# The last two multiplications on the keys and rates of an RWKV-7 scan, on GpSimd instead of VectorE

## The chip, the cores and the metric

One core of a Trainium2 chip runs the whole program. The metric is the device time of one execution in microseconds. TensorE (PE) runs the matrix products, VectorE (DVE), ScalarE (ACT) and GpSimd (POOL) the rest, and each engine works through its own instructions in order. SyncE (SP) issues most transfers. Engines wait for each other by semaphores.

## The reference

The program is one step of a two-layer model for 128 context tokens and 512 latent tokens of width 1024. Layer 0 mixes by HGRN2 and RG-LRU, layer 1 by RWKV-7; a mixture of experts ends each layer. The change is in RWKV-7's recurrence, which runs forwards and backwards in time:

```
w  = exp(-exp(-0.5) * sigmoid(w_in));  a = sigmoid(a_in)
kd = k * (1 + (a - 1) * k_a)
step:  sa = S @ (-kk_t)
       S  = S * w_t + sa (kk_t * a_t)^T + v_t kd_t^T
       o_t = S @ r_t
```

## The kernel before, in words

The recurrence is computed in chunks of 128 tokens: 5 chunks (128 context, 4 x 128 latent) for 4 groups of 4 heads, which makes 20 scan steps, n = 0 to 19, each for both directions d = 0 and 1. A step's operands are [128 x 256] tiles in SBUF, one row for each channel of a pair of heads.

For step n the code forms the running sum of the log decays, moves it so that half of the chunk's decay lies on each side (`hb`, the step's centre), and takes exponentials of it on ACT (`E1`, `E2`, `E3`). From them come four operands: the keys `KP` = kd * `E2`, the rates `BE` = kk * a * `E2`, and the two halves of `KR`, kk * `E3` and r * `E1`. `bonus_operands` (L2059) makes kd in place of the decay sum (`KD`, L2065) and the bonus term `SQ` (L2069, twice). `decayed_operands` (L2071) then multiplies `KP` (L2076), `BE` (L2077) and the two halves of `KR` (L2079, L2080), and the last of these raises `unit_ready`.

PE uses them in `rate_products`: for each direction a PSUM tile `AR` = `BE` x `KR` (16 matmuls of 128 x 256 for the two directions, in half tiles of 64 channels), then the small tile `BN` from `SQ`. `KP` x `KR` gives `BR` a little later. DVE copies `AR` out under a mask in `rates_out` (L2111), SP writes it to DRAM and reads its 16x16 diagonal blocks back, GpSimd inverts those (L742 to L752, a chain of 32 small operations each waiting for the one before), SP stores and reloads the inverses, and PE goes from 16 to 128 in three levels (tiles `G`, `D`, L1107 waits for the first load).

The order of the work is written out by hand. In its loop, PE does for step n: `rate_products(n + 1)`, level 4 of step n, `BR`, the levels 5 and 6, then the outputs `OT`. DVE does in step n: `rates_out(n + 1)`, masks and levels of step n, between them the operands of step n + 2, at the end `bonus_operands` and `decayed_operands` of n + 2 for d = 0 and d = 1, then `outputs_taken(n)` (L2174 to L2183), and from group 1 on the normalisation of the group before (L2097 to L2103). So what DVE makes at the end of step n is what PE wants at the very start of step n + 1. PSUM is a ring of four tiles: a tile can be opened when the tile four places before it has been read out. The `AR` tile of d = 0 is four places before the second `G` tile of level 4.

Of the kernel before, what the change touches and what calls it, by code (L numbers as in the profile page):

```python
# [86 lines left out]
def scan_step(n):  # L87

    return divmod(n, NCH) if n < NGRP * NCH else None


def step_name(n):
    g, st = divmod(n, NCH)
    return f"_{g}_{st}"
# [66 lines left out]
def build(nc, A, const, outs, xspill, slots_in, slots_out):  # L161
# [3 lines left out]
    ALU = mybir.AluOpType  # L165
# [5 lines left out]
    with ctx:  # L171
# [28 lines left out]
        def vcol(name, i, n=1):  # L200
            return VT[:, VB[name] + i:VB[name] + i + n]
# [12 lines left out]
        def small(n):  # L214
# [36 lines left out]
            "lru_rows", "lru_sent", "f_log", "b_ready", "head_diff", "head_exp", "head_ready",  # L251
            "lvl_diff", "lvl_exp", "lvl_q", "lvl_k", "st_in", "s_final", "s_final_sent", "on_root", "o_a_ready",
            "chosen", "routed", "zero_ready", "zero_filled", "slots_filled", "over_done", "x_parked", "x_back", "xi_ready", "lora_in", "rw_st_in", "rw_clear", "scr_clear", "tri_in", "tri_out",
            "kk_sq", "gates_exp", "kk_norm", "decay_sum", "decay_exp", "unit_ready", "kb_t", "fin_out",
            "rhs_out", "r0_ready", "n_out", "gates_clamped", "gates_done", "ctx_state", "ctx_state_sent", "scan_done", "gn_centred", "gn_sq", "gn_var", "gn_root",
            "z_ready", "silu_out", "acc_ready", "y_sent")}
        pool_chain = sem("pool_chain")
# [156 lines left out]
        R1 = Rf.rearrange("p (k t) -> p k t", k=KT)  # L414
# [16 lines left out]
        STR = []  # L431
# [11 lines left out]
        for d in range(2):  # L443
            z = {}
# [25 lines left out]
        def square(a):  # L470
            return a.rearrange("p (i k) -> p i k", k=TB)

        def turned(a):
            return a.rearrange("p (i k) -> p k i", k=TB)
# [171 lines left out]
        def _(pool):  # L646
# [85 lines left out]
            def link(ins):  # L732
                n_chain[0] += 1
                ins.then_inc(pool_chain, 1)
                pool.wait_ge(pool_chain, n_chain[0])

            for n in range(NGRP * NCH):
                pool.wait_ge(S["tri_in"], 32 * (n + 1))
                if n:
                    for d in range(2):  # L740
                        pool.wait_ge(tri_stored[d], 32 * n)
                link(nc.gpsimd.tensor_copy(square(triL[0:NB_T]), turned(triX[0:NB_T])))  # L742
                link(nc.gpsimd.tensor_scalar(triR, triL, -1.0, None, ALU.mult))
                link(nc.gpsimd.memset(triR[:, 0::TB + 1], 1.0))
                r3, l3 = square(triR), square(triL)
                for k in range(1, TB - 1):
                    m = TB - 1 - k
                    prod = triX[:, 0:m * k].rearrange("p (i c) -> p i c", c=k)
                    link(nc.gpsimd.tensor_tensor(prod, l3[:, k + 1:, k:k + 1].broadcast_to([2 * NB_T, m, k]),
                                                 r3[:, k:k + 1, 0:k].broadcast_to([2 * NB_T, m, k]), ALU.mult))  # L750
                    link(nc.gpsimd.tensor_tensor(r3[:, k + 1:, 0:k], r3[:, k + 1:, 0:k], prod, ALU.subtract))
                nc.gpsimd.tensor_copy(square(triRT), turned(triR)).then_inc(S["tri_out"], 1)  # L752
            moe(1)


        @block.tensor
        def _(pe):
            nxt = [0]

            def open_tile(n):  # L760
                assert n == nxt[0], (n, nxt[0])
                nxt[0] += 1
                if n >= RING_P:
                    pe.wait_ge(psum_free[n % RING_P], n // RING_P)
                return tile(n)
# [173 lines left out]
            for i in range(3):  # L939
                ins = nc.tensor.transpose(ps[:, i * P:(i + 1) * P], vrow[:, i * P:(i + 1) * P], ident)  # L940
            done(ins)
            pe.wait_ge(S["x_in"], 32)
            for k in range(KT):
                ps = open_tile(T["xT"] + k)
                for c in range(NCH):
                    ins = nc.tensor.transpose(ps[:, c * P:(c + 1) * P], xtok[:, c, k * P:(k + 1) * P], ident)
# [14 lines left out]
            for u in range(8):  # L961
                c, d = u // 2, u % 2
# [120 lines left out]
            def rate_products(n):  # L1083
                for d in range(2):
                    z = STR[d]
                    pe.wait_ge(S["unit_ready"], 2 * n + d + 1)
                    ps = open_tile(T["AR" + step_name(n)] + d)
                    done(head_products(ps, z["BE"][n % 2], z["KR"][n % 3]))
                ps = open_tile(T["BN" + step_name(n)])
                for d in range(2):  # L1090
                    for j in range(UC):
                        c0 = HG * d + 2 * j
                        ins = mm(ps[:, c0:c0 + 2], STR[d]["SQ"][:, j * P:(j + 1) * P], hsel)
                done(ins)
# [168 lines left out]
        def _(act):  # L1263
# [231 lines left out]
            def decay_exps(n, d):  # L1495
                z = STR[d]
                h0 = 4 * (n % 3) + 2 * d
                act.wait_ge(S["decay_sum"], 2 * n + d + 1)
                A_(em[:, h0:h0 + 2], hb[:, h0:h0 + 2], ACT.Exp, scale=-W_DECAY)
                A_(z["E1"], z["B"], ACT.Exp, scale=-W_DECAY)  # L1500
                A_(z["E2"], z["B"], ACT.Exp, scale=W_DECAY)
                A_(z["E3"], z["E3"], ACT.Exp, scale=-W_DECAY).then_inc(S["decay_exp"], 1)
# [78 lines left out]
        def _(dve):  # L1581
# [445 lines left out]
            def sum_decays(n, d):  # L2027

                z = STR[d]
                h0 = 4 * (n % 3) + 2 * d  # L2030
                dve.wait_ge(S["gates_done"], 2 * n + d + 1)
                one = half_one[:, 0:1].broadcast_to([P, P])
                for j in range(UC):
                    js = slice(j * P, (j + 1) * P) if d == 0 else slice((j + 1) * P - 1, j * P - 1 if j else None, -1)
                    ins = nc.vector.tensor_tensor_scan(z["B"][:, js], one, z["LA"][:, js], 0.0, ALU.mult, ALU.add)
                link(ins)
                e0 = P - 1 if d == 0 else 0
                link(TS(hb[:, h0:h0 + 2], z["B"][:, e0::P], 0.5, None, ALU.mult))
# [20 lines left out]
            def bonus_operands(n, d):  # L2059

                g, st = scan_step(n)
                z, ch = STR[d], chunk_of(st, d)
                ts, cg = slice(ch * P, (ch + 1) * P), slice(UC * g, UC * (g + 1))
                dve.wait_ge(S["decay_exp"], 2 * n + d + 1)
                link(TT(c3(z["KD"]), K1[:, cg, ts], c3(z["KP"][n % 2]), ALU.mult))  # L2065
                for j in range(UC):
                    ct = UC * g + j
                    js = slice(j * P, (j + 1) * P)
                    STT(z["SQ"][:, js], R1[:, ct, ts], vcol("rw_rk", ct), z["KD"][:, js], ALU.mult, ALU.mult)  # L2069

            def decayed_operands(n, d):  # L2071

                g, st = scan_step(n)
                z, ch = STR[d], chunk_of(st, d)
                ts, cg = slice(ch * P, (ch + 1) * P), slice(UC * g, UC * (g + 1))
                TT(z["KP"][n % 2], z["KD"], z["E2"], ALU.mult)  # L2076
                TT(z["BE"][n % 2], z["BE"][n % 2], z["E2"], ALU.mult)  # L2077
                kr = z["KR"][n % 3].rearrange("p (j a t) -> p j a t", j=UC, a=2)
                TT(kr[:, :, 0, :], c3(z["KK"]), c3(z["E3"]), ALU.mult)  # L2079
                TT(kr[:, :, 1, :], R1[:, cg, ts], c3(z["E1"]), ALU.mult).then_inc(S["unit_ready"], 1)  # L2080
# [251 lines left out]
```

## Time and profile before

| | us |
|---|---|
| three runs | 2650.51, 2660.67, 2659.58 |
| their median | 2659.58 |
| the profiled execution | 2647.23 |
| its span, first to last instruction | 2645.4 |
| PE busy | 2155.2 (81%) |
| DVE busy | 1062.1 (40%) |
| ACT busy | 684.7 (26%) |
| GpSimd busy | 351.2 (13%) |
| mean granted TensorE clock | 0.896 of full speed |

The scan takes some 750 us of the span, from 1415 to about 2170 us, and there a step takes about 35 us. A row of a timeline is one instruction or a run of equal ones: its start, its length, the engine, the line of the code, the operation with its output and inputs, and in brackets how long the engine had been idle and what ended that. Matmuls show the line of the helper that issues them, L776. PEclk is the TensorE clock that was granted, as a share of full speed: 1.00 is 2.4 GHz, 0.50 is 1.2 GHz.

### The profile page before, as it was taken

The numbers are of one execution on the slowest core, as the hardware profiler recorded it, in microseconds if no ns is written. First come the engines' busy times: TensorE is split into PE (matmuls) and PEld (weight loads), VectorE is DVE, ScalarE is ACT, GpSimd is POOL, SyncE is SP. The second block draws the span as 40 slices with busy tenths as digits, with TensorE's granted clock in tenths as the row PEclk, the third lists the DMA queues.
The fourth block names the chain that finished last, engine by engine and source line by source line (L and its number), as shares of the span: only waits on it lengthen the run. The fifth ranks groups of instructions, "written<-read, shape, count | busy, mean of one in ns | idle before, by whom it ended". The sixth has DMA issues, their size and how long they took to land.

```text
span 2645.4 us, 29905 instructions
## 1 busy us (share of the span) xinstructions
PE 2155.2 (81%) x11858; PEld 1601.5 (61%) x11858; DVE 1062.1 (40%) x2278; ACT 684.7 (26%) x1402; POOL 351.2 (13%) x816
## 2 busy tenths in 40 slices
PE   6999990777885997369995999999999989759964
PEld 3554560444564674135574898888888875546742
DVE  2246221666132110271003577777777753311104
ACT  1254221222130110030003244444444421301112
POOL 3000001232001000100002122233222210010001
PEclk9999995888977998679997699999999999779987
DMA  8124319333144995421101222221222231449943
GB/s 261 48 96 159 120 62 398 114 128 119 46 144 163 344 343 183 151 88 64 64 32 33 54 52 58 50 55 40 54 55 55 48 107 33 143 172 346 343 149 127
DMA packets 328505, 337.12 MB, mean 127 GB/s; under 512 B 76836, under 2 KB 296208, under 8 KB 327856
## 3 DMA queue, kind: packets, MB, share of 16 engines
q1 hardware_dynamic: 308496, 262.61, 31.8%
q0 software_dynamic: 11984, 40.63, 4.1%
q10 hardware_dynamic: 7888, 31.99, 3.0%
q8 instruction: 95, 1.56, 0.2%
q14 instruction: 42, 0.34, 0.0%
HBM read 259.67 MB, written 75.51 MB: 127 GB/s over the span
## 4 chain that ended last, share of the span: by engine, by line
PE 71%; DVE 14%; ACT 5%; DMA 3%; issue 2%; POOL 2%; ACTq 2%; SPq 1%; POOLq 0%; DVEq 0%
PE psum_ring L776 65%; PE psum_ring L1098 2%; PE psum_ring L860 1%; DMA arena<-expert_inputs 1%; ACTq L1397 1%; ACT h_normed L1292 1%; ACTq L1394 1%; DVE arena L2069 1%; PE psum_ring L1180 1%; POOL expert_inputs L697 1%; POOL arena L709 1%; DMA arena<-expert_outputs,arena 0%; PE psum_ring L932 0%; ACT arena L1307 0%; DVE h_normed L2183 0%
## 5 line engine op out<-in xcount | busy, mean ns | idle before, releaser
L776 PE MATMUL psum_ring<-arena 128*128 128x256 f32 (+5 forms) x3440 | 645.9, 359 | 57.4 <-ACT arena L1307 18.2
L776 PEld LDWEIGHTS psum_ring<-arena 128*128 128x128 f32 (+1 forms) x3440 | 490.9, 196 | 167.9 <-issue 75.5
L776 PE MATMUL psum_ring<-arena,weight_ring 128*128 128x64 f32 (+3 forms) x1792 | 367.7, 391 | 21.4 <-DVE arena L2080 15.8
L776 PEld LDWEIGHTS psum_ring<-arena,weight_ring 128*128 128x128 f32 (+1 forms) x1792 | 245.9, 204 | 132.4 <-issue 103.8
L776 PE MATMUL psum_ring<-h_normed,weight_ring 128*128 128x512 f32 (+1 forms) x768 | 211.6, 437 | 5.8 <-ACT h_normed L1292 5.8
L776 PEld LDWEIGHTS psum_ring<-h_normed,weight_ring 128*128 128x128 f32 x768 | 117.7, 192 | 98.8 <-issue 98.8
L776 PE MATMUL psum_ring<-weight_ring,small 128*2 128x256 f32 x768 | 175.8, 387 | 0.3
L860 PE MATMUL psum_ring<-consts,arena 128*128 128x128 f32 x350 | 55.2, 295 | 105.1 <-DMA arena<-expert_inputs 102.3
L776 PE MATMUL psum_ring<-x_resid,weight_ring 128*128 128x512 f32 (+1 forms) x480 | 111.8, 390 | 25.7 <-DVE x_resid L2002 25.7
L776 PEld LDWEIGHTS psum_ring<-weight_ring,small 128*2 128x2 f32 x768 | 63.8, 86 | 101.4 <-issue 9.4
L860 PEld LDWEIGHTS psum_ring<-consts,arena 128*128 128x128 f32 x350 | 46.9, 154 | 127.0 <-DMA arena<-expert_inputs 105.0
L776 PEld LDWEIGHTS psum_ring<-x_resid,weight_ring 128*128 128x128 f32 x480 | 70.9, 199 | 65.2 <-issue 65.2
L1739 DVE COPY arena<-psum_ring 128x1024 f32<-128x1024 f32 x32 | 39.2, 1224 | 163.0 <-PE psum_ring L860 162.9
L776 PE MATMUL psum_ring<-h_normed 128*128 128x128 f32 x190 | 29.5, 309 | 87.4 <-DVE h_normed L1957 67.8
L1747 DVE TENSOR_TENSOR arena<-arena,psum_ring 128x256 f32<-128x256 f32 x32 | 13.5, 421 | 205.2 <-ACT arena L1317 205.2
L1317 ACT ACTIVATE arena<-psum_ring 128x256 f32<-128x256 f32 x32 | 12.3, 383 | 297.5 <-PE psum_ring L776 297.5
L776 PE MATMUL psum_ring<-arena,x_resid 128*128 128x64 f32 (+1 forms) x624 | 86.9, 274 | 0.2 <-DVE arena L2023 0.2
L1276 ACT ACTIVATE h_normed<-x_resid 128x640 f32<-128x640 f32 x40 | 28.7, 734 | 211.1 <-DVE x_resid L1636 205.0
L776 PEld LDWEIGHTS psum_ring<-h_normed 128*128 128x128 f32 x190 | 25.7, 213 | 92.8 <-issue 92.3
L2133 DVE TENSOR_TENSOR arena<-psum_ring,consts 128x256 f32<-128x256 f32 x120 | 49.4, 422 | 78.0 <-PE psum_ring L776 77.4
L1636 DVE SCALAR_TENSOR_TENSOR x_resid<-psum_ring,modulation,x_resid 128x128 f32<-128x128 f32 x64 | 31.6, 545 | 122.1 <-PE psum_ring L776 120.6
L776 PEld LDWEIGHTS psum_ring<-arena,x_resid 128*128 128x128 f32 x624 | 80.0, 195 | 0.3 <-issue 0.3
(361 smaller groups left out, 3142.5 us busy)
## 6 DMA issues: line engine op xcount, KB each, us to landing
arena<-in_moe_w SPq DMA_DIRECT2D x105, 1024.0 KB, 10.7
weight_ring<-in_w_mod SPq DMA_DIRECT2D x48, 1024.0 KB, 5.2
arena<-expert_inputs SPq DMA_DIRECT2D x35, 512.0 KB, 7.3
expert_outputs<-arena POOLq DMA_DIRECT2D x32, 512.0 KB, 7.7
weight_ring<-in_ab_w_in SPq DMA_DIRECT2D x14, 1024.0 KB, 5.0
expert_inputs<-arena ACTq DMA_DIRECT2D x1, 12800.0 KB, 36.4
expert_outputs<-arena ACTq DMA_DIRECT2D x1, 12800.0 KB, 67.3
weight_ring<-expert_outputs SPq DMA_DIRECT2D x20, 512.0 KB, 4.6
```

Of the source, the lines that this page charges most:

```text
L697: pool.indirect_dma_start(slots_in, bass.IndirectOffsetOnAxis(ap=PI[:, j * NCH + c:j * NCH + c + 1], axis=0), HTOK[:, c, :], None).then_in ...
L709: pool.indirect_dma_start((G0, G1)[j][:, c, :], None, slots_out, bass.IndirectOffsetOnAxis(ap=PI[:, j * NCH + c:j * NCH + c + 1], axis=0)) ...
L776: return nc.tensor.matmul(out, lhsT, rhs, start=start, stop=stop)
L860: ins = nc.tensor.transpose(ps[:, k * P:(k + 1) * P], src[:, k * P:(k + 1) * P], ident)
L1098: ins = nc.tensor.transpose(ps[:, c0 + hl * P:c0 + (hl + 1) * P], src[:, hl * P:(hl + 1) * P], ident)
L1180: ins = nc.tensor.transpose(ps[:, c0:c0 + P], STR[d][key][n % 2][:, j * P:(j + 1) * P], ident)
L1276: A_(H[:, k, :], X[:, k, :], ACT.Square).then_inc(S["sq_ready"], 1)
L1292: A_(H[:, k, a:b], H[:, k, a:b], ACT.Identity, scale=coef[i][:, 2 * k + s:2 * k + s + 1], bias=MOD[:, layer, shift + k, s:s + 1]).then_inc ...
L1394: act.dma_start(dst.rearrange("(a p) d -> p a d", p=P), ZERO.unsqueeze(1).broadcast_to([P, NE + N_OVER, D])).then_inc(S["zero_filled"], 16)
L1636: ins = STT(X[:, k, a:b], ps[:, a:b], MOD[:, layer, gate + k, s:s + 1], X[:, k, a:b], ALU.mult, ALU.add)
L1739: free(nc.vector.tensor_copy(XGT[e % 2], ps), n)
L2133: free(TT(STR[d]["G"].rearrange("p (h c) -> p h c", c=HD), ps[:, 0:HG * HD].rearrange("p (h c) -> p h c", c=HD), gm, ALU.mult), tn)
```

## The change

The multiplications that make `KP` and `BE` leave DVE's `decayed_operands`. GpSimd gets a function `decayed_keys(n)` that waits for the new semaphore `bonus_out` (raised by DVE's last bonus product of step n, direction d), multiplies `KP` and `BE` by `E2`, and raises the new semaphore `decayed`. It stands once ahead of GpSimd's loop, for step 0, and then behind the inverse of step n, for step n + 1. PE waits for `decayed` beside `unit_ready` ahead of each `AR` tile. ACT and DVE wait for `decayed` of the step before where they overwrite `E2` and `KD`.

```diff
+            def decayed_keys(n):
+                if scan_step(n):
+                    for d in range(2):
+                        z = STR[d]
+                        pool.wait_ge(S["bonus_out"], 2 * n + d + 1)
+                        nc.gpsimd.tensor_tensor(z["KP"][n % 2], z["KD"], z["E2"], ALU.mult)
+                        nc.gpsimd.tensor_tensor(z["BE"][n % 2], z["BE"][n % 2], z["E2"],
+                                                ALU.mult).then_inc(S["decayed"], 1)
+            decayed_keys(0)
             for n in range(NGRP * NCH):
...
                 nc.gpsimd.tensor_copy(square(triRT), turned(triR)).then_inc(S["tri_out"], 1)
+                decayed_keys(n + 1)
...
                     pe.wait_ge(S["unit_ready"], 2 * n + d + 1)
+                    pe.wait_ge(S["decayed"], 2 * n + d + 1)
...
                 act.wait_ge(S["decay_sum"], 2 * n + d + 1)
+                if n:
+                    act.wait_ge(S["decayed"], 2 * n + d - 1)
...
                 dve.wait_ge(S["gates_done"], 2 * n + d + 1)
+                if n:
+                    dve.wait_ge(S["decayed"], 2 * n + d - 1)
...
-                    STT(z["SQ"][:, js], R1[:, ct, ts], vcol("rw_rk", ct), z["KD"][:, js], ALU.mult, ALU.mult)
+                    ins = STT(z["SQ"][:, js], R1[:, ct, ts], vcol("rw_rk", ct), z["KD"][:, js], ALU.mult, ALU.mult)
+                ins.then_inc(S["bonus_out"], 1)
...
-                TT(z["KP"][n % 2], z["KD"], z["E2"], ALU.mult)
-                TT(z["BE"][n % 2], z["BE"][n % 2], z["E2"], ALU.mult)
```

On DVE, at the end of a scan step, the operands of a later step for d = 0 and the first instruction for d = 1 stood before as follows (L2065 is `KD`, L2069 `SQ`, L2076 `KP`, L2077 `BE`, L2079 and L2080 `KR`):

```order
L2065 TENSOR_TENSOR arena<-arena,weight_ring 128x256 [waits decay_exp]
L2069 SCALAR_TENSOR_TENSOR arena<-arena,vectors 128x128 [waits dve_chain]
L2069 SCALAR_TENSOR_TENSOR arena<-arena,vectors 128x128
L2076 TENSOR_TENSOR weight_ring<-arena 128x256
L2077 TENSOR_TENSOR weight_ring<-weight_ring,arena 128x256
L2079 TENSOR_TENSOR arena<-arena 128x2x128
L2080 TENSOR_TENSOR arena<-arena 128x2x128
L2065 TENSOR_TENSOR arena<-arena,weight_ring 128x256 [waits decay_exp]
```

The same place of DVE after the change, where the lines have moved by 16 or 17 (L2082 is `KD`, L2086 `SQ`, L2095 and L2096 `KR`):

```order
L2082 TENSOR_TENSOR arena<-arena,weight_ring 128x256 [waits decay_exp]
L2086 SCALAR_TENSOR_TENSOR arena<-arena,vectors 128x128 [waits dve_chain]
L2086 SCALAR_TENSOR_TENSOR arena<-arena,vectors 128x128
L2095 TENSOR_TENSOR arena<-arena 128x2x128
L2096 TENSOR_TENSOR arena<-arena 128x2x128
L2082 TENSOR_TENSOR arena<-arena,weight_ring 128x256 [waits decay_exp]
```

Two instructions of each direction are gone from DVE's row, and the rest keeps its order.

On GpSimd, the end of the inverse of step 0 and the beginning of that of step 1 stood before as follows (L752 is the last copy of an inverse, L742 the first of the next):

```order
L751 TENSOR_TENSOR weight_ring<-weight_ring 64x14 [waits pool_chain]
L752 COPY weight_ring<-weight_ring 64x256 [waits pool_chain]
L742 COPY weight_ring<-weight_ring 32x256 [waits tri_stored1,tri_stored0,tri_in]
L743 TENSOR_SCALAR weight_ring<-weight_ring 64x256 [waits pool_chain]
L744 MEMSET weight_ring 64x16 [waits pool_chain]
```

The same place of GpSimd after the change, with L743 and L744 now the multiplications of `KP` and `BE`, for d = 0 and then d = 1:

```order
L762 TENSOR_TENSOR weight_ring<-weight_ring 64x14 [waits pool_chain]
L763 COPY weight_ring<-weight_ring 64x256 [waits pool_chain]
L743 TENSOR_TENSOR arena<-arena 128x256 [waits bonus_out]
L744 TENSOR_TENSOR arena<-arena 128x256
L743 TENSOR_TENSOR arena<-arena 128x256 [waits bonus_out]
L744 TENSOR_TENSOR arena<-arena 128x256
L753 COPY weight_ring<-weight_ring 32x256 [waits tri_stored1,tri_stored0,tri_in]
```

The four multiplications of step 1 stand between the inverse of step 0 and that of step 1.

## Rows read from the trace of the kernel before

**Rows 1.** The chain that ended last (page, part 4), by engine

```profile
PE 71%; DVE 14%; ACT 5%; DMA 3%; issue 2%; POOL 2%; ACTq 2%; SPq 1%; POOLq 0%; DVEq 0%
```

**Rows 2.** Windows (us, busy PE PEld DVE ACT POOL, PEclk, DMA share, GB/s)

```profile
1490.00:1520.00 30.00, 29.40 (x150) 27.31 (x149) 17.55 (x45) 8.31 (x23) 0.12 (x1) 0.56 0.09 20
1580.00:1610.00 30.00, 28.46 (x253) 26.84 (x252) 21.07 (x53) 15.21 (x40) 9.60 (x32) 1.00 0.23 54
```

**Rows 3.** Waits of PE, 1640 to 2140 us (us, times, longest)

```profile
PE psum_ring L776 <- DVE arena L2111: 8.7, 7, 1.7
PE psum_ring L776 <- DVE weight_ring L2111: 5.7, 6, 1.2
...
PE psum_ring L776 <- DVE arena L2080: 2.5, 3, 0.8
```

**Rows 4.** Timeline of DVE from 2109 us (start us, us, line, operation, tiles)

```profile
2109.75 0.62 DVE L2069 SCALAR_TENSOR_TENSOR arena<-arena,vectors 128x128 f32<-128x128 f32 x2
2110.29 0.42 DVE L2076 TENSOR_TENSOR arena<-arena 128x256 f32<-128x256 f32 x1
...
2111.30 0.41 DVE L2080 TENSOR_TENSOR arena<-arena 128x256 f32<-128x256 f32 x1
...
2113.61 0.42 DVE L2080 TENSOR_TENSOR arena<-arena 128x256 f32<-128x256 f32 x1
...
2117.50 1.22 DVE L2111 TENSOR_TENSOR arena<-psum_ring,consts 128x1024 f32<-128x1024 f32 x1
```

**Rows 5.** Timeline of PE in the same stretch

```profile
2113.76 2.00 PE L776 MATMUL psum_ring<-arena 64*128 64x256 f32 x16
...
2118.86 1.08 PE L776 MATMUL psum_ring<-weight_ring 128*128 128x64 f32 x8 [1.18 <-DVE arena L2111]
```

**Rows 6.** Timeline of PE at the first step of a group

```profile
1824.84 1.13 PE L776 MATMUL psum_ring<-arena 64*128 64x256 f32 x8 [0.82 <-DVE arena L2080]
...
1828.41 1.08 PE L776 MATMUL psum_ring<-weight_ring 128*128 128x64 f32 x8 [0.52 <-DVE arena L2111]
```

**Rows 7.** GpSimd's multiplications of layer 0, line 687 (ns min/median/max)

```profile
L687 POOL TENSOR_TENSOR h_normed<-h_normed,arena x19: 852/863/5882, 453.2 to 654.0; 128x320 f32<-128x320 f32 x19
```

**Rows 8.** Timeline of GpSimd and DVE in layer 0, at 452 us

```profile
451.89 0.82 DVE L1949 TENSOR_TENSOR arena<-arena 128x640 f32<-128x640 f32 x1 [53.19 <-ACT small L1412]
...
453.19 1.03 POOL L687 TENSOR_TENSOR h_normed<-h_normed,arena 128x320 f32<-128x320 f32 x1 [187.24 <-ACT h_normed L1418]
453.23 1.67 DVE L1949 TENSOR_TENSOR arena<-arena 128x640 f32<-128x640 f32 x1
...
454.18 1.58 POOL L688 TENSOR_TENSOR h_normed<-h_normed,arena 128x320 f32<-128x320 f32 x1
454.82 1.48 DVE L1950 TENSOR_TENSOR h_normed<-h_normed,arena 128x512 f32<-128x512 f32 x1
```

**Rows 9.** Timeline of the same two engines at 510 us

```profile
510.05 0.82 DVE L1949 TENSOR_TENSOR arena<-arena 128x640 f32<-128x640 f32 x1
510.15 5.88 POOL L687 TENSOR_TENSOR h_normed<-h_normed,arena 128x320 f32<-128x320 f32 x1 [26.23 <-ACT h_normed L1418]
...
514.33 0.82 DVE L1957 TENSOR_TENSOR h_normed<-h_normed,arena 128x640 f32<-128x640 f32 x1
```

**Rows 10.** Timeline at the start of the scan, several engines

```profile
1432.97 3.78 PE L776 MATMUL psum_ring<-arena,weight_ring 64*128 64x256 f32 x16 [14.20 <-DVE arena L2080]
...
1456.72 0.68 POOL L752 COPY weight_ring<-weight_ring 64x256 f32<-64x256 f32 x1
1456.86 0.83 DVE L2076 TENSOR_TENSOR arena<-arena 128x256 f32<-128x256 f32 x1
...
1456.99 3.84 PE L776 MATMUL psum_ring<-arena 64*128 64x256 f32 x16 [14.47 <-DVE arena L2080]
...
1464.00 4.03 PE L776 MATMUL psum_ring<-weight_ring 128*128 128x64 f32 x16 [1.38 <-DMA weight_ring<-expert_outputs]
```

**Rows 11.** Window of 2 us behind a wait of PE, as Rows 2

```profile
2081.00:2083.00 2.00, 2.00 (x11) 1.80 (x12) 1.45 (x5) 0.00 (x0) 0.00 (x0) 0.50 0.70 212
```

More of the change, by code:

```diff
@@ L253, in build @@
             "chosen", "routed", "zero_ready", "zero_filled", "slots_filled", "over_done", "x_parked", "x_back", "xi_ready", "lora_in", "rw_st_in", "rw_clear", "scr_clear", "tri_in", "tri_out",
-            "kk_sq", "gates_exp", "kk_norm", "decay_sum", "decay_exp", "unit_ready", "kb_t", "fin_out",
+            "kk_sq", "gates_exp", "kk_norm", "decay_sum", "decay_exp", "unit_ready", "kb_t", "fin_out", "bonus_out", "decayed",
             "rhs_out", "r0_ready", "n_out", "gates_clamped", "gates_done", "ctx_state", "ctx_state_sent", "scan_done", "gn_centred", "gn_sq", "gn_var", "gn_root",
```

## The prediction

> **What bounds the kernel now.** I read the chain of waits first. PE is 71% of it and DVE 14% [rows 1], so a microsecond of DVE counts only where PE waits for it. The windows come next: in a scan step at full clock PE is busy 28.46 of 30 us, and there are stretches at half clock where it is busy throughout [rows 2]; nothing on DVE matters in those. The list of PE's waits then shows where DVE is late at the point that the change touches: 8.7 + 5.7 = 14.4 us in 13 waits for L2111, the masked copy that frees an `AR` tile, and 2.5 us in 3 waits for L2080, the last operand [rows 3]. Over 20 steps the whole place is worth 17 us, 0.6% of the program, if the clock is left aside.
>
> The timeline of one step shows how the two hang together [rows 4, 5]. DVE makes the operands of d = 0 and d = 1 without a gap, the last ending at 2113.61 + 0.42 = 2114.03. PE begins the `AR` products at 2113.76; its 16 matmuls take 2.00 us, so those of d = 1 begin 1.00 us later, at 2114.76, and find their operands 0.73 us old. The operands are not what PE waits for. But behind them on DVE stand the outputs, the normalisation and L2111 at 2117.50, and for that one PE waits 1.18 us at 2118.86. DVE has no pause of its own choice in this stretch but one for ACT, so a microsecond more or less ahead of the outputs moves L2111 by as much. This is the form of the steps from group 1 on. At the first step of a group PE arrives sooner: it waits 0.82 us for L2080 itself and then 0.52 us for L2111 [rows 6]. In the steps of group 0 no normalisation stands in between, and neither wait is there.
>
> **What the change takes away.** Four multiplications a step leave DVE (two for each direction). Starts 2110.29 and 2111.30 are three instructions apart [rows 4], so one costs 0.335 us and four 1.34 us.
>
> **What it adds.** Four multiplications a step on GpSimd, of 128x256. The trace shows none of that size there; the nearest row is layer 0's multiplication of 128x320, 863 ns in the middle [rows 7]. By size that is 863 x 256/320 = 690 ns. The bounds of one are 0.69 us by itself and 5.88 us, the longest of that row.
>
> Where these stand is the question, since GpSimd works while DVE makes the other operands. Layer 0 shows the two side by side [rows 8]. DVE's L1949 of 128x640 takes 0.82 us alone and 1.67 us when GpSimd's multiplication has started 0.04 us ahead of it; GpSimd's next takes 1.58 instead of 0.86 while DVE has its turn. So each stands still while the other runs, and they take turns. The same is seen in the scan: GpSimd's copy L752 runs from 1456.72 to 1457.40, and DVE's multiplication that comes in at 1456.86 takes 0.83 instead of 0.42 us [rows 10]. A GpSimd multiplication thus costs DVE 1.67 - 0.82 = 0.85 us at 320 columns, by size 0.68 at 256; I take 0.66, since the part that does not read is no bar.
>
> The Trainium skill says the same on its page "SBUF — State Buffer", section "Who interferes with whom": a VectorE instruction with two inputs in SBUF shares its second read port with GpSimd, and whichever starts first holds it for the whole instruction. Rows 8 agree (0.85 us lost). By that rule alone the order of starting decides, which is the forecast below; rows 9 speak against it, and are a rival.
>
> **DVE's stretch.** `bonus_out` of d = 0 comes at 2109.75 + 0.62 = 2110.37 in the step shown. GpSimd has been idle since its inverse, so nothing is queued ahead. It takes turns with the two rate products of d = 0, with L2065 and L2069 of d = 1, and, once `bonus_out` of d = 1 is there, with the two of d = 1. Three of its four multiplications fall among these; the fourth falls beside the outputs, whose other input is in PSUM, and I cost it at nothing to DVE (if that cover fails it is 0.66 a step more). DVE's stretch becomes 3 x 0.66 - 1.34 = +0.64 us longer. Its bounds are -1.34 (no blocking) and 4 x 0.66 - 1.34 = +1.30.
>
> **PE's new wait.** The last multiplication ends about 0.60 us behind DVE's last operand (0.69 less the 0.09 by which DVE's instructions overlap): 2114.03 + 0.64 + 0.60 = 2115.27. PE wants it at 2114.76, so the second half of `AR` is 0.51 us late. Queued behind that wait are all of PE's own matmuls; L2111 waits for the first half only.
>
> **The sum, step by step** (the operands of step i are used in step i - 1):
> - i = 0 and 1, the filling. The `AR` of step 0 begins with the operands, at 1432.97 [rows 10]. GpSimd's turns push its second half from about 1434.9 to 1435.5, +0.6, and the inverse of step 0 with it. The four multiplications of step 1 now stand behind this inverse: from 1457.40 + 0.6 they need 4 x 0.69 = 2.8 us, to 1460.8, where PE had begun at 1456.99. Level 4 began only at 1464.00, released by the transfer of the inverses, and moves by 0.6 anyhow; the late half of `AR` (1.92, half of 3.84) ends at 1462.7, which leaves 1.9 for the small tile `BN`, about what it takes. I put +0.7.
> - i = 2 lies in the half-clock stretch of rows 2: nothing.
> - i = 3 to 5, group 0: 0.51 each, +1.5.
> - i = 6: PE waited for L2080 and no L2111 follows: 0.64 + 0.60 = +1.2.
> - i = 11 and 16: +1.24 at `AR`, of which the later wait of 0.52 takes up part: +0.7 each, +1.4.
> - the other 11 from i = 7 on: 0.51 is hidden in the wait for L2111, which grows by 0.64: 11 x 0.64 = +7.0.
>
> Together +11.8 us. Then the clock. Behind 6 of the 13 waits for L2111 the granted clock fell to half within about 2 us and stayed there for some 3.4 us or more; one such window shows PE busy all of it at 0.50 [rows 11]. A fall costs about half of its length, 1.7 us. In the steps of group 0, with waits under 1 us, there was none. With waits longer by half I take two falls more, +3.4; the bounds are none and 7 x 1.7 = +12.
>
> The sum is +15.2 us: 2647.23 becomes 2662.4 for the profiled execution. That execution is 12.4 us under the median 2659.58 of the runs shown, so against the median I forecast 2675.
>
> **Rivals.**
> - *DVE keeps the port.* At 510 us GpSimd's multiplication came in 0.10 us behind the start of a DVE instruction and took 5.88 us: it ran only when DVE's unbroken run ended at 514.33 + 0.82 = 515.15 [rows 9]. `bonus_out` arrives in the same way, just behind the start of a rate product. Then DVE goes on until it has a gap, which is behind L2065 of d = 1, where it waits for its own result. Two multiplications fall in there and the rest behind the operands: 2 x 0.66 - 1.34 = 0 for DVE. The late half of `AR` remains: 1.5 + 1.2 + 1.4 + 0.7 = +4.8, or 2664. For it: rows 9. Against: rows 8 and 10, where GpSimd got in between two DVE instructions.
> - *They run beside each other.* If 128x256 multiplications do not block, DVE's stretch is 1.34 us shorter and the operands are early. The 14.4 us of L2111 waits go but for some 0.8, the three waits of 0.82 shrink by 0.4 each, and six falls of the clock (10 us) go with them: -25, or 2635. For it: DVE stands between PE and the next step there. Against: every row in which both read SBUF.
> - *It costs more.* GpSimd is held up at every turn and the clock falls behind each of the 13 waits: +11.8 + 12, or with 1.30 a step (7.3 more) up to +31: 2683 to 2691.
> - *The change does nothing where it stands*: 2660, if the falls of the clock at half speed cover the place in most steps, as in i = 2. Rows 2 show that full clock is the rule; I put this with the first rival.
>
> **How the numbers follow.** About 0.5%, 13 us, is what a measurement can tell from no change: under 2646 is faster, over 2673 slower. The forecast has 0.54 (2664 to 2688: 0.32 slower, 0.22 the same), DVE keeping the port or nothing 0.20 (0.18 the same, 0.02 slower), beside each other 0.14 (all faster but 0.01), costing more 0.12 (slower). That is 0.13 faster, 0.41 the same, 0.46 slower. The range of 8 in 10 reaches from 2645, about where the third case begins to be left out, to 2691.
>
> **What would show it.** In the trace after, DVE's `KR`, `KD` and `SQ` beside GpSimd should take about 0.66 us longer than 0.42 or 0.35, three times a step, and the outputs begin some 0.6 us later against `KD`. GpSimd's multiplications should take 0.7 us, or 1.0 where they wait. PE's `AR` of d = 1 should wait for GpSimd by 0.5 us, at the first step of a group by 2 us, and the waits for L2111 should be nearer to 1.8 than to 1.2. It is wrong if DVE's instructions keep their 0.42 us; then the second case holds if the waits for L2111 are gone, and the first if GpSimd's first multiplication takes over 1.2 us.

## The result, and the profile after

The changed kernel took 2684.91 us in the median of 4 runs (2674.27 to 2691.43), the kernel before 2658.43 in 4 (2650.51 to 2660.67). The ratio is 1.0101, with a 95% interval of 1.0062 to 1.0140. It is slower by 26.5 us; the forecast was slower, 2675 in a range of 2645 to 2691. The profiled execution took 2674.27 us, 27.0 above the 2647.23 of the one before; the differences below are made between these two.

I read GpSimd first: did the turns come? Its timeline in a late step (start us, us, engine, line, operation, tiles, and in brackets the idle time and what ended it):

```profile
2132.11 0.84 POOL L743 TENSOR_TENSOR arena<-arena 128x256 f32<-128x256 f32 x1 [10.74 <-DVE arena L2086]
2132.91 0.90 POOL L744 TENSOR_TENSOR arena<-arena 128x256 f32<-128x256 f32 x1
2134.82 0.84 POOL L743 TENSOR_TENSOR arena<-arena 128x256 f32<-128x256 f32 x1 [1.01 <-DVE arena L2086]
2135.62 0.90 POOL L744 TENSOR_TENSOR arena<-arena 128x256 f32<-128x256 f32 x1
```

L743 makes `KP` and L744 `BE`, for d = 0 and then d = 1. The same stretch on DVE, which answers to [rows 4] (L2082 was L2065, L2096 was L2080, L2127 was L2111):

```profile
2130.96 0.42 DVE L2082 TENSOR_TENSOR arena<-arena 128x256 f32<-128x256 f32 x1
...
2131.94 0.42 DVE L2095 TENSOR_TENSOR arena<-arena 128x256 f32<-128x256 f32 x1
2132.28 0.95 DVE L2096 TENSOR_TENSOR arena<-arena 128x256 f32<-128x256 f32 x1
2133.15 0.94 DVE L2082 TENSOR_TENSOR arena<-arena 128x256 f32<-128x256 f32 x1
...
2134.66 0.42 DVE L2095 TENSOR_TENSOR arena<-arena 128x256 f32<-128x256 f32 x1
2135.00 0.95 DVE L2096 TENSOR_TENSOR arena<-arena 128x256 f32<-128x256 f32 x1
2135.87 0.57 DVE L2193 TENSOR_TENSOR arena<-arena,psum_ring 64x128 f32<-64x128 f32 x2
...
2139.41 1.22 DVE L2127 TENSOR_TENSOR arena<-psum_ring,consts 128x1024 f32<-128x1024 f32 x1
```

Three DVE instructions take 0.94 or 0.95 us instead of 0.42: each begins 0.17 to 0.24 us behind a GpSimd multiplication and stands still until that has ended. The fourth multiplication, at 2135.62, lies beside L2193, whose second input is in PSUM, and that one is not longer. So it is three of four, as forecast, at 0.53 us each and not 0.66. From the start of the first L2082 to the end of the last L2096 are 4.99 us. In the step of [rows 4] these were 4.73, from 2109.30 to the 2114.03 at which the last L2080 ended:

```profile
2109.30 0.42 DVE L2065 TENSOR_TENSOR arena<-arena 128x256 f32<-128x256 f32 x1
```

DVE's stretch has grown by 0.26 us.

PE in the same stretch, which answers to [rows 5]; first its products, then the loads of their weights:

```profile
2135.42 2.35 PE L788 MATMUL psum_ring<-arena 64*128 64x256 f32 x16
...
2140.78 1.08 PE L788 MATMUL psum_ring<-weight_ring 128*128 128x64 f32 x8 [1.08 <-DVE arena L2127]
```

```profile
2135.41 0.73 PEld L788 LDWEIGHTS psum_ring<-arena 64*128 64x128 f32 x8
2136.60 0.76 PEld L788 LDWEIGHTS psum_ring<-arena 64*128 64x128 f32 x8 [0.45 <-issue]
```

The `AR` products take 2.35 instead of 2.00 us, since the second half waits for GpSimd's last multiplication, which ends at 2135.62 + 0.90 = 2136.52. The profile puts this down to "issue". The wait for L2127 is 1.08, not longer than the 1.18 of before: the copy is 0.26 us later, but so is PE, by 0.35.

The waits of PE from 1640 to 2140 us [rows 3] are 13.8 us now, less than the 16.9 of before, in a kernel that is 27 us slower; they aren't the measure of the loss:

```profile
PE psum_ring L788 <- DVE weight_ring L2127: 5.5, 5, 1.1
PE psum_ring L788 <- DVE arena L2127: 4.3, 5, 1.1
PE psum_ring L788 <- DVE arena L2096: 4.0, 3, 1.6
```

At the first step of a group [rows 6] PE's new wait is longest. PE:

```profile
1646.65 1.14 PE L788 MATMUL psum_ring<-arena,weight_ring 64*128 64x256 f32 x8
1649.37 1.13 PE L788 MATMUL psum_ring<-arena,weight_ring 64*128 64x256 f32 x8 [1.58 <-DVE arena L2096]
```

GpSimd:

```profile
1648.36 0.90 POOL L744 TENSOR_TENSOR weight_ring<-weight_ring,arena 128x256 f32<-128x256 f32 x1
```

The wait has gone from 0.82 to 1.58 us. L2096 is named, but it ended at 1648.68; what came last is GpSimd's L744, at 1649.26. With two semaphores ahead of one matmul the name in brackets need not be the right one: compare the ends. What follows is in the windows of 2 us (us, busy PE, PEld, DVE, ACT, POOL, PEclk, DMA share, GB/s), as [rows 11]:

```profile
1648.00:1650.00 2.00, 0.63 (x6) 0.66 (x8) 2.00 (x4) 0.00 (x0) 1.27 (x2) 1.00 0.00 0
1650.00:1652.00 2.00, 2.00 (x15) 1.67 (x11) 1.70 (x2) 0.00 (x0) 0.00 (x0) 0.67 0.27 81
1652.00:1654.00 2.00, 2.00 (x11) 2.00 (x11) 0.36 (x3) 1.73 (x6) 0.00 (x0) 0.50 0.66 183
...
1660.00:1662.00 2.00, 2.00 (x16) 2.00 (x15) 0.61 (x1) 0.82 (x2) 1.53 (x7) 0.77 0.00 0
```

Behind the wait the granted clock goes from 2.4 to 1.2 GHz and comes back at 1661. And this is where the time is. In page part 2 each digit is 1/40 of the span, in tenths, and the scan is digits 22 to 33. Before:

```profile
PEclk9999995888977998679997699999999999779987
```

After:

```profile
PEclk9999995988977998679996799899997999769987
```

The digits are coarse; the 31st shows it best, 9 before and 7 after. To count it, I cut the scan from 1520 us to its end into windows of 2 us and add up (1 - PEclk) x 2: the time that the clock took. The scan's end is PE's first product of the stage behind it, at 2172.38 us before and 2197.33 after, 24.95 later, which is nearly all of the 27.0 by which the execution is longer. The clock took 17.5 us before and 44.3 us after, 26.8 more; PE's idle time in the same stretch is 46.1 and 45.5. The two are not independent (a step at half clock hides DVE's delay), so this doesn't say that the direct cost is 0.2. That is read from steps without a fall. PE's product behind L2038 comes once a step:

```profile
1890.91 1.30 PE L788 MATMUL psum_ring<-arena 128*128 128x128 f32 x10 [0.94 <-DVE arena L2038]
...
1926.34 1.52 PE L788 MATMUL psum_ring<-arena 128*128 128x128 f32 x12 [0.94 <-DVE arena L2038]
```

The same product in two rows of the kernel before, where the line was L2023:

```profile
1699.59 0.63 PE L776 MATMUL psum_ring<-arena 128*128 128x128 f32 x4 [0.94 <-DVE arena L2023]
1734.76 1.52 PE L776 MATMUL psum_ring<-arena 128*128 128x128 f32 x12 [0.94 <-DVE arena L2023]
```

That is 35.43 us against 35.17, +0.26 a step, what DVE's stretch has gained. In the steps of group 0 without a fall it is +0.36 (34.12 against 33.76). With one short fall such a step is 36.8 us before and 37.0 after. From 1630 us on the clock falls in 7 of 13 steps before and in 12 of 13 after, and in some of these for longer.

The start of the scan [rows 10] shows a turn of another kind:

```profile
1457.23 3.54 DVE L2095 TENSOR_TENSOR arena<-arena 128x256 f32<-128x256 f32 x1
1457.74 0.71 POOL L743 TENSOR_TENSOR arena<-arena 128x256 f32<-128x256 f32 x1
...
1459.23 3.92 PE L788 MATMUL psum_ring<-arena 64*128 64x256 f32 x16 [15.47 <-issue]
1459.78 0.71 POOL L744 TENSOR_TENSOR arena<-arena 128x256 f32<-128x256 f32 x1
...
1464.43 1.10 PE L788 MATMUL psum_ring<-weight_ring 128*128 128x64 f32 x8 [0.29 <-DMA weight_ring<-expert_outputs]
```

Four multiplications follow each other without a gap behind the inverse, and a DVE instruction of 0.42 us, which came in at 1457.23, stands still until the last of them has ended at 1459.78 + 0.71 = 1460.49; it ends 0.28 later, at 1460.77, as those above did. PE's products come 2.2 us later than before, but level 4, which waits for a transfer, moves only from 1464.00 to 1464.43.

### The profile page after: what moved, and what is told of

It is laid out like the page before. It is cut to its first block, busy times and chain, and to the rows that moved or that the text cites. A ratio compares the mean times of both kernels' runs of the same rounds, so it can differ in the third digit from the quotient of the medians.

```text
span 2672.4 us, 29980 instructions
## 1 busy us (share of the span) xinstructions
PE 2180.6 (82%) x11858; PEld 1622.6 (61%) x11858; DVE 1069.4 (40%) x2198; ACT 685.0 (26%) x1402; POOL 418.7 (16%) x896
## 4 chain that ended last, share of the span: by engine, by line
PE 72%; DVE 13%; ACT 4%; DMA 3%; issue 2%; POOL 2%; ACTq 2%; SPq 1%; DVEq 0%; POOLq 0%
PE psum_ring L788 66%; PE psum_ring L1111 2%; PE psum_ring L872 1%; DMA arena<-expert_inputs 1%; ACTq L1410 1%; ACT h_normed L1305 1%; ACTq L1407 1%; DVE arena L2096 1%; POOL arena L709 1%; DVE arena L2086 1%; PE psum_ring L1193 1%; POOL expert_inputs L697 1%; DVE arena L2082 1%; PE psum_ring L944 0%; ACT arena L1320 0%
## 5 line engine op out<-in xcount | busy, mean ns | idle before, releaser
L788 PE MATMUL psum_ring<-arena 128*128 128x256 f32 (+5 forms) x3440 | 662.6, 367 | 58.5 <-ACT arena L1320 18.2
L788 PEld LDWEIGHTS psum_ring<-arena 128*128 128x128 f32 (+1 forms) x3440 | 505.1, 202 | 172.1 <-issue 94.9
```

Source lines behind the costliest of these rows:

```text
L788: return nc.tensor.matmul(out, lhsT, rhs, start=start, stop=stop)
```

## The experiments

Two theories stood after this. A: the change delays DVE and PE by a quarter of a microsecond a step, and the rest of the 27 us is the clock falling behind PE's pauses. B: the work on GpSimd costs the 27 us by itself (turns, or PE's wait for GpSimd). All times are medians of the runs; the ratio is against runs of the kernel before on the same chip and isn't simply that of the two medians. Kernels that ran on different chips are compared by their ratios. Single runs of one kernel lie up to 35 us apart (those before, 2638 to 2673 on one chip), so a difference under some 5 us isn't told apart.

**Keys alone, late.** GpSimd multiplies `KP` only, once DVE's last operand is there, so that the two never meet; `BE` goes back to DVE; PE waits for `decayed` only ahead of `BR`, which is where `KP` is needed.

```diff
-pool.wait_ge(S["bonus_out"], 2 * n + d + 1)
+pool.wait_ge(S["unit_ready"], 2 * n + 2)
 nc.gpsimd.tensor_tensor(KP ...).then_inc(S["decayed"], 1)
-nc.gpsimd.tensor_tensor(BE ...)          # and on DVE again
-pe.wait_ge(S["decayed"], ...)            # ahead of AR; now ahead of BR
```

> GpSimd multiplies the keys KP alone, and only when DVE's last operand of both directions is done (it waits for unit_ready of d = 1); the rates BE stay on DVE; PE waits for the keys ahead of BR. Theory 1 (the two engines block each other at the shared port, PE waits for DVE): no DVE instruction is stretched, GpSimd's take 0.71 us, DVE's stretch is 2 x 0.335 = 0.67 us shorter, the waits of PE for L2080 (0.82) and L2111 (1.18) shrink by as much, about -10 us, and fewer falls of the clock (17.5 us lost before) take off 0 to 12 more: 2636 to 2648 us, ratio 0.992 to 0.996. Rival (work of GpSimd in this place is itself what costs, by the clock or otherwise): not faster than before, 2660 or more.

2641.84 us, ratio 0.9966 (0.9932 to 1.0000): not slower, and only just apart from no change. The multiplication takes its own time, 0.73 us (ns min/median/max):

```profile
L743 POOL TENSOR_TENSOR weight_ring<-arena x20: 715/726/730, 1434.5 to 2071.3; 128x256 f32<-128x256 f32 x20
```

and the waits of PE from 1640 to 2140 us (us, times, longest), which answer to [rows 3], are 8.3 us instead of 16.9:

```profile
PE psum_ring L786 <- DVE arena L2126: 5.2, 7, 1.3
PE psum_ring L786 <- DVE weight_ring L2126: 2.8, 6, 0.5
PE psum_ring L786 <- DVE arena L2095: 0.3, 2, 0.2
```

So two multiplications a step taken off DVE, and put where they block nothing, shorten PE's waits by 8.6 us in 13 steps, 0.66 each. That the clock would gain with them was a miss: in the profiled run it took 29.0 us to the scan's end, 11.5 more than in the kernel before, mostly around a group's first steps; steps without a fall are 34.59 us, 0.57 shorter than before. Over all runs the mean granted clock is 0.894 in the middle, against 0.893 of the kernel before on that chip.

**Keys alone, beside DVE.** The same with the early signal: `KP` waits for `bonus_out` as in the changed kernel. PE's `AR` doesn't wait for GpSimd here.

```diff
-pool.wait_ge(S["unit_ready"], 2 * n + 2)
+pool.wait_ge(S["bonus_out"], 2 * n + d + 1)
```

> GpSimd multiplies the keys KP alone, at once behind bonus_out as in the change; the rates BE stay on DVE; PE waits for the keys ahead of BR, not ahead of AR. Theory 1 (blocking stretches DVE by 0.53 us a time): two DVE instructions a step take 0.95 instead of 0.42 us, DVE's stretch is 2 x 0.53 - 0.67 = 0.39 us longer than before, about as in the change (0.26), while PE never waits for GpSimd at AR. If DVE's delay is what lets the clock fall: as slow as the change but for PE's own wait, 2672 to 2685 us. Rival (the wait of PE for GpSimd at AR lets the clock fall): +5 us and no more falls than before, 2660 to 2667.

2683.92 us, ratio 1.0098 (1.0068 to 1.0128): all of the loss without PE's new wait. Two DVE instructions a step take 0.95 us; DVE's stretch is 5.12 us (2138.84 to 2143.96), where it was 4.06 in the kernel above (2066.49 to 2070.55) and 4.73 before:

```profile
2140.16 0.95 DVE L2094 TENSOR_TENSOR arena<-arena 128x256 f32<-128x256 f32 x1
```

PE's waits are twice those of the kernel above, 17.0 us, but no more than the 16.9 of the kernel before; the clock fell in each of the 13 steps and took 72.1 us in the profiled run, which was the slowest of six:

```profile
PE psum_ring L786 <- DVE weight_ring L2126: 7.3, 6, 1.6
PE psum_ring L786 <- DVE arena L2126: 7.0, 5, 1.8
PE psum_ring L786 <- DVE arena L2095: 2.7, 3, 1.2
```

Between these two kernels only the time of GpSimd's start differs, and it is worth 42 us by the medians, 35 by the ratios.

**More work on DVE, none on GpSimd.** The kernel before with one more multiplication of the same size for each direction, into a scratch tile, 0.67 us a step.

```diff
 TT(z["KP"][n % 2], z["KD"], z["E2"], ALU.mult)
+TT(z["G"], z["KD"], z["E2"], ALU.mult)
```

> The kernel before, with one more 128x256 multiplication on DVE for each direction, into a scratch tile, in front of the others: DVE's stretch is 0.67 us longer and GpSimd has nothing to do with it. Theory 1 with the clock (longer waits of PE, whoever causes them, let the granted clock fall more often): waits for L2080 1.5 and for L2111 1.85 us, +9 us by themselves and 10 to 25 us lost to the clock beyond the 17.5 of before: 2678 to 2695 us. Rival (the falls come of GpSimd's work): +9 us alone, 2667, with the clock as before.

2682.16 us, ratio 1.0109 (1.0046 to 1.0172). The waits are 24.3 us:

```profile
PE psum_ring L776 <- DVE arena L2112: 10.9, 7, 1.8
PE psum_ring L776 <- DVE weight_ring L2112: 8.7, 6, 1.7
PE psum_ring L776 <- DVE arena L2081: 4.7, 5, 1.5
```

GpSimd isn't needed for such a loss: a late DVE is enough. By its waits alone it would be 7.4 us (24.3 - 16.9). The clock fell in 11 of the 13 steps and took 32.4 us, 14.9 more than before, though the profiled run was the fastest of four, 2660.27; the others go up to 2697.21. This speaks against B; the fill below decides it.

**The changed kernel with PE kept busy.** Products of the identity by itself, which nothing reads, in the pauses ahead of `AR` of d = 1 (3, in a group's first step 12) and ahead of level 4 (9).

```diff
+def fill(ps, m):
+    for i in range(m):
+        mm(ps[:, 512 + 128 * (i % 4):640 + 128 * (i % 4)], ident, ident)
...
+                        fill(ps, 12 if n % NCH == 1 else 3)   # rate_products, d = 1
...
+                        fill(ps, 9)                           # level_products, lv == 4, d == 0
```

> The changed kernel; PE does matmuls of the identity by itself, into columns of a tile that are overwritten or not read, where it waits: 3 ahead of the wait for d = 1 of AR (12 in the first step of a group) and 9 ahead of the first G tile of level 4 from group 1 on. Theory (PE's waits there let the clock fall, and the falls are nearly all of what the change costs): the clock lost in the scan from 1520 us on goes from 44 us to under 12, and the time to 2645 to 2658 us in spite of the added matmuls. Rival (the falls come of something else than PE's pause, or the time is lost in DVE's stretch): no faster than the change, 2680 to 2692.

2672.58 us, ratio 1.0068 (1.0044 to 1.0092). The clock was lost for 5.1 us only, as A has it, but the time missed its range of 2645 to 2658: I had sized the fill wrongly. One product is two PE instructions and 0.25 us, and nine of them take 2.25 us in a pause of 1.1:

```profile
1766.55 2.25 PE L788 MATMUL psum_ring<-consts 128*128 128x128 f32 x18
```

**The fill in its size.** The same in three kernels, counted by their own pauses: ahead of `AR` of d = 1 in a group's first step, ahead of level 4, and 2 products ahead of the layout change of the outputs (`N6`), a pause of 0.60 us in each step.

```diff
+if d and n > NCH and n % NCH == 1: fill(ps, 3)        # before; 5 in the changed kernel; 0 in keys late
+if lv == 4 and d == 0 and n > NCH: fill(ps, {0: 2, 1: 6}.get(n % NCH, 4))
+                                                      # changed: 4; keys late: 2, in a group's second step 5
+fill(turned, 2)                                       # N6
```

The kernel before:

> The kernel before, with small multiplications of the identity by itself (0.25 us each on PE) in three of PE's pauses of a step: 3 ahead of the second direction's A matmuls in a group's first step, 4 (2 and 6 in a group's first two steps) ahead of the fourth-level solve, 2 ahead of the layout change of the outputs. Nothing reads them. Theory (the falls of the granted clock follow PE's pauses, and they alone scatter and lengthen the scan): the time lost to the clock from 1520 us to the scan's end falls from 17.5 us to 8 or less, and the time is 2638 to 2648, 0.2 to 0.6% below the kernel before. Rival (the falls come from something else, or PE is the bound without its pauses): the lost clock stays at 15 or more and the time is 2650 to 2665 by what the fill adds.

The changed kernel:

> The changed kernel with the same fill, sized for its own pauses (5, 4 and 2). Theory (the change costs 0.26 to 0.35 us a step by itself and the rest through the clock): the lost clock falls from 44 us to 10 or less, the time is 2645 to 2658, and what is left above the filled kernel before is 5 to 12 us. Rival (the work moved to GpSimd costs the 27 us by itself, in the engines' turns): the time stays at 2675 to 2690 and 25 us above the filled kernel before.

Keys alone, late:

> The kernel in which GpSimd multiplies the keys alone, late, and PE waits for it ahead of the readout, with the fill (none, 2 or 5, and 2). Theory: its steps without a fall are 0.5 us shorter at the A matmuls than those of the kernel before, so with the falls gone it is 6 to 10 us below the filled kernel before, 2625 to 2638, under both kernels. Rival (its pauses at the group's starts, where its clock falls, aren't those that are filled here): 2638 to 2645, as without the fill.

They took 2638.47, 2645.08 and 2633.51 us; ratios 0.9937 (0.9910 to 0.9965), 0.9971 (0.9946 to 0.9996) and 0.9917 (0.9891 to 0.9943). By the ratios the changed kernel with the fill is 1.3% faster than without, some 35 us, and it is 6.6 us above the filled kernel before. That is far from the 25 us that B wanted: B falls. Its scan from 1520 us to the end, and that of the changed kernel without fill ahead of it:

```profile
1520.00:2197.33 677.33, 631.83 (x5140) 590.48 (x5139) 466.71 (x1119) 286.84 (x767) 232.99 (x644) 0.93 0.22 52
```

```profile
1520.00:2170.29 650.29, 626.10 (x5302) 589.75 (x5300) 461.35 (x1109) 283.76 (x757) 230.21 (x629) 0.97 0.23 54
```

PE executes more instructions, is busy for 5.7 us less, and the scan ends 27 us earlier. Steps without a fall are 35.16 us in the filled kernel before (1731.10 to 1766.26 at the product of each step named above) and 35.42 in the filled changed one (1734.46 to 1769.88): again +0.26. The clock took 8.5 us in the first, where I expected 8 or less, and 17.1 in the second, where I expected 10 or less: both misses, the second a clear one; both times were hits. So the 6.6 us hold some of the clock's time too. The third beats both kernels, by 17 us against the kernel before on the same chip, but by less against the filled kernel before (5 us) than the 6 to 10 expected; its clock took 17.1 us.

**Which pause?** The fill of the changed kernel in parts: ahead of level 4 alone; the two others without it; each of these two alone; and only at the two places where the change itself made PE wait (1 product ahead of `AR` of d = 1 in each step, 5 in a group's first).

Level 4 alone:

> The changed kernel with the fill ahead of the fourth-level solve alone (4 in each step, about 1.0 us in its wait of 1.08 us); the two other pauses stay as they are. Theory A (the clock falls behind the longest single pause of a step): nearly all of the filled kernel's gain, 2645 to 2655, lost clock 25 us or less. Theory B (it falls with the sum of a step's pauses, whichever they are): a share of it by the time filled, 1.0 of about 1.6 us a step, 2655 to 2665.

The two others:

> The changed kernel with the two other fills alone (5 ahead of the second direction's A matmuls in a group's first step, 2 ahead of the outputs' layout change in each step), and the wait of 1.08 us ahead of the fourth-level solve left empty. Theory A: little of the gain, 2675 to 2685, lost clock 35 us or more. Theory B: the rest of it, 2662 to 2674.

A group's first steps alone:

> The changed kernel with the fill in the wait of a group's first step alone: 5 small multiplications ahead of the second direction's A matmuls in three steps of the scan, 3.75 us of PE in all. The fill without the fourth-level wait gave 27 us, and the long stretches at 1.2 GHz begin right behind these waits of 1.58 us. Theory (these three waits, which the change doubled, set off the long stretches): most of the 27 us, 2657 to 2668, lost clock 36 us or less. Rival (the short pause of 0.55 us in each step does it): 2675 to 2685.

The layout change alone:

> The changed kernel with the fill ahead of the outputs' layout change alone (2 in each step, in a pause of 0.55 us). Theory (the group's first waits set off the long stretches): little, 2673 to 2683. Rival: most of the 27 us, 2657 to 2668.

`AR` of d = 1 in each step:

> The changed kernel with the fill only where the change itself put PE's new pauses: ahead of the second direction's A matmuls, 1 small multiplication in each step (0.45 us idle there) and 5 in a group's first step (1.58 us). The pauses that the kernel before has too (0.94, 0.60 and 1.1 us) stay empty. Theory (the clock falls by what the change adds to PE's pauses): the time comes back to that of the kernel before plus the change's own 5 to 7 us, 2655 to 2668. Rival (once a step has so much of pauses, which of them the falls follow is set by their place; the one ahead of the outputs' layout change gave back 16 us, this one gives less): 2670 to 2680, as with the group's first steps alone.

The lost clock is of the profiled run, which is one execution, and is counted to the scan's end; the ratio and the mean granted clock of the whole program (its median) are of all the runs:

```
filled                      median us   ratio (95%)               mean clock  clock lost, us
nothing (the change)        2684.91     1.0101 (1.0062 - 1.0140)  0.882       44.3
level 4                     2676.99     1.0089 (1.0069 - 1.0108)  0.886       58.0
group's first steps         2678.74     1.0096 (1.0060 - 1.0131)  0.885       39.3
AR of d = 1, each step      2673.14     1.0070 (1.0040 - 1.0100)  0.887       58.0
layout change               2668.45     1.0044 (1.0019 - 1.0069)  0.890       44.4
layout change, first steps  2658.26     1.0027 (1.0010 - 1.0045)  0.893       34.2
all three                   2645.08     0.9971 (0.9946 - 0.9996)  0.900       17.1
```

The kernel before has a mean clock of 0.892 to 0.894 on these chips. Over the runs the time follows the mean clock, which the single execution of the last column doesn't show.

Theory A of these expectations, that the longest pause does it, fell at once: level 4, the longest in a common step, gives back 0.1% of the 1.3%. Theory B, that it goes by the sum of the pauses, wanted 2655 to 2665 there and missed too; with the two others A's 2675 to 2685 is out, and the 2658.26 lies below B's 2662 to 2674. That the three first steps do it fell as well (0.05%); the layout change alone gives 0.6%, 2668.45, just above its rival's 2657 to 2668. And filling most of what the change had added (one product of 0.25 us in 0.45 us, five in 1.58) doesn't bring the kernel back; there the rival's 2670 to 2680 held. No single pause carries the 27 us. Whether the parts add up isn't told: 0.7% for the two and 0.1% for level 4 stand against 1.3% for all three, with intervals of 0.2 to 0.4% either way on each.

With level 4 alone two kinds of fall come apart. Windows of the first two steps of a group, then of the steps behind them; first the changed kernel without fill, then with level 4 filled:

```profile
1656.00:1692.00 36.00, 34.45 (x232) 32.59 (x232) 20.51 (x51) 14.06 (x37) 12.88 (x36) 0.74 0.15 34
1700.00:1830.00 130.00, 120.25 (x999) 111.89 (x998) 93.48 (x229) 59.95 (x161) 49.40 (x140) 0.95 0.22 49
```

```profile
1656.00:1692.00 36.00, 34.40 (x178) 32.84 (x178) 20.87 (x52) 11.39 (x31) 5.45 (x11) 0.57 0.15 36
1700.00:1830.00 130.00, 123.15 (x1064) 116.42 (x1060) 96.81 (x240) 61.94 (x168) 48.72 (x137) 0.99 0.22 52
```

The falls that take 1.7 us, most of them in the common steps, are nearly gone (2 in the scan instead of 9), and the longer ones, most of them near the start of a group, take 54.6 us instead of 29.0. So in these two executions the wait ahead of level 4 goes with the first kind, and the long stretches have another origin, which no run shows. The longer falls took clearly less only where several fills stood together: 22.2 us with the layout change and the first steps, 15.4 with all three, against 27.3 to 54.6 in the other three.

## Why the prediction was right, and where its sizes were off

- **That they take turns.** Right, at three meetings a step and none at the outputs. The Trainium skill, "SBUF — State Buffer", section "Who interferes with whom", has whichever starts first holding the port for its instruction; the trace agrees in the last 18 of the 20 steps, the 0.95 us against 0.42; in the second step DVE lost more than one instruction of GpSimd's, the 3.54 us at 1457.23. The rival of DVE keeping the port is out: GpSimd's multiplications took 0.84 and 0.90 us, at most 0.91. The rival of no blocking is out too. (The first rival's +4.8 held DVE's 0.64 at three first steps, although DVE's stretch stays as it was in it; nothing hangs on that.)
- **The price of a turn**, 0.66 us, was too high: 0.53. I had scaled the 0.85 of a 320 column multiplication by size; a multiplication is 0.71 by itself, and DVE's instruction comes 0.17 us into it, so that some 0.54 are left to wait. DVE's stretch grew by 0.26, not 0.64.
- **PE's new wait**: 0.45 at the weights, 0.35 in the products, where 0.51 was forecast; 1.58 at a group's first step, where 0.82 + 1.24 = 2.06 was. In group 0, where 0.51 a step was forecast, the steps without a fall are 0.36 longer. Right in kind, smaller by the same turns.
- **The wait for L2111** was to grow from 1.2 to about 1.8. It shrank to 1.08. The step that failed is "0.51 is hidden in the wait": the late half delays PE itself, and with DVE's delay smaller, PE comes no sooner to the copy than before. It made no difference to the sum.
- **The direct sum**, +11.8, was twice too much: 0.26 a step is about 5 us over 20 steps, an estimate; with the pauses filled in both kernels the difference is 6.6, some of it still the clock's.
- **The clock** is the term that was mis-sized the other way: +3.4 for two falls more, within 0 and 12; the falls took 26.8 us more, outside these bounds. I had tied them to the waits for L2111, 13 of them, and to their length. But the waits didn't grow, and the falls did, and the long stretches behind a group's first steps, up to 8.5 us lost in one, had no term at all. The kernel before already spoke against the length: of these two waits the first has no fall behind it and the second has one, and of its 17.5 us 5.1, at 1840 us, stand behind none of the 13.

```profile
2044.41 1.07 PE L776 MATMUL psum_ring<-weight_ring 128*128 128x64 f32 x8 [1.75 <-DVE arena L2111]
2008.49 1.53 PE L776 MATMUL psum_ring<-x_resid 128*128 128x64 f32 x8 [0.52 <-DVE weight_ring L2111]
```

The two errors partly cancelled: +15.2 forecast, +27 measured. So the direction came by the mechanism that was named, and that the size fell into the range was in part luck. The case "it costs more" had the right total, 2683 to 2691, and a part of the right reason.
- **Open**: why 0.25 us a step more of pauses, 2.97 instead of 2.72 (0.94, 0.60, 1.08 and 0.35 against 0.94, 0.60 and 1.18), makes the clock fall in 12 steps of 13 instead of 7. The fills show that the loss goes with the pauses; what sets off a fall was not found. The length of a wait doesn't tell it (1.75 us without a fall, 0.52 with one), and neither does the list of waits, in which a step at half clock shows less.

## What to carry to other kernels

Multiplications moved from VectorE to GpSimd shorten nothing here where both engines then read SBUF at the same time: each meeting costs a turn (0.53 us), where an instruction taken away saves 0.335. Move work only to a stretch where the other engine rests. Where PE is the bound and its clock falls in places, price a delay of a few tenths of a microsecond by the falls that it may set off, not by its own length. Before moving work at all, try to fill PE's pauses with products that nothing reads, sized by their measured duration: here that was worth 12 us by the medians (0.6% by the ratio) to the kernel before and 1.3%, some 35 us, to the changed one, while a fill of 2.25 us in a pause of 1.1 gave most of its gain away.

## What the runs showed that I had not expected

- GpSimd's four multiplications in a row stretch a DVE instruction of 0.42 us to 3.54 (at 1457.23), the mirror of [rows 9], where DVE's run stretched GpSimd's to 5.88. In the later steps, where instructions of the two come in turn, each DVE instruction loses 0.53.
- The same work on GpSimd, begun some 3.0 us later for d = 0 and 1.1 for d = 1, makes 42 us of difference (2683.92 against 2641.84).
- PE with 162 instructions more in the trace of the scan (5302 against 5140) ends it 27 us earlier (650.29 us against 677.33).
